# Recurrence of a diffusion step: decay factors made at a job's head, keys and queries projected first, their rotation spread over three jobs

## What is computed

```
h    = x * (1 + scale) + shift                 # adaLN
proj = h @ w_in                                # 1024 -> 3584 columns
o_a  = differential attention of q, k, v       # q, k of the 512 tokens rotated (2-D axial)
o_b  = gelu(u) * (w_s @ layer_norm(gelu(v)))   # spatial gating, u and v from proj
o_c  = gated linear recurrence, two directions # below
x    = layer_norm(ALPHA * x + gate * (concat(o_a, o_b, o_c) @ w_out))
x    = layer_norm(ALPHA * x + gate * top-2 of 16 experts(x modulated))
```

```
o_t   = (q_t * exp(b_t)) @ S + sum over s <= t of (q_t * exp(b_t - b_s)) . k_s  i_s
S_new = exp(b_last) * S + sum over s of (k_s * exp(b_last - b_s)) i_s
```

## Time and profile before

| | |
|---|---|
| runs shown (us) | 2160.1, 2160.1, 3152.97; median 2160.1 |
| profiled execution | 2148.85 us, span 2147.0 us, mean granted clock 0.93 |
| busy share of the span | PE 85%, PEld 44%, DVE 34%, ACT 18%, POOL 14% |
| recurrence of the first layer | 134.8 to 407.5 us |
| recurrence of the second layer | 1176 to 1455 us |

### The profile page before, as it was taken

How to read it: one execution, slowest core, us unless ns; L and a number is a source line. 1 busy time by engine, 2 the same in 40 slices (tenths; PEclk the granted TensorE clock), 3 DMA queues, 4 the chain that set the end, 5 groups by cost and what they waited for, 6 DMA issues and landing times. The chain is left out here.

```text
span 2147.0 us, 20618 instructions
## 1 busy us (share of the span) xinstructions
PE 1825.3 (85%) x7528; PEld 939.9 (44%) x7528; DVE 736.3 (34%) x1179; ACT 379.5 (18%) x699; POOL 302.7 (14%) x348
## 2 busy tenths in 40 slices
PE   3998888787984999999799898877879399999993
PEld 1464544544552443344345455445544344434441
DVE  0035465366453111111150555545635511101105
ACT  1323112143110000000141421212420100000001
POOL 0011125400000000000130222271000000000005
PEclk9999999899985999999899999988989589999997
DMA  9321111364117877799603012107320496897943
GB/s 368 132 95 40 46 45 40 138 246 178 68 59 267 319 265 296 287 363 396 231 16 134 1 44 86 40 1 261 119 78 30 148 370 220 309 382 266 397 159 147
DMA packets 142087, 380.44 MB, mean 177 GB/s; under 512 B 9732, under 2 KB 15876, under 8 KB 135332
## 3 DMA queue, kind: packets, MB, share of 16 engines
q1 hardware_dynamic: 111840, 292.31, 36.3%
q10 hardware_dynamic: 21108, 55.36, 7.1%
q0 software_dynamic: 9040, 31.46, 4.0%
HBM read 343.65 MB, written 35.45 MB: 177 GB/s over the span
## 5 line engine op out<-in xcount | busy, mean ns | idle before, releaser
L847 PE MATMUL psum<-sb_arena 128*128 128x512 f32 (+1 forms) x1248 | 494.2, 596 | 10.4 <-DMA sb_arena<-w_up 9.0
L577 PE MATMUL psum<-sb_wA,sb_arena 128*128 128x512 f32 x800 | 379.4, 625 | 0.0
L847 PEld LDWEIGHTS psum<-sb_arena 128*128 128x128 f32 (+1 forms) x1248 | 192.9, 172 | 269.2 <-issue 257.3
L847 PE MATMUL psum<-sb_wA,sb_arena 128*128 128x512 f32 (+1 forms) x672 | 273.7, 604 | 7.1 <-DMA sb_wA<-w_up 4.4
L577 PEld LDWEIGHTS psum<-sb_wA,sb_arena 128*128 128x128 f32 x800 | 154.0, 200 | 173.6 <-issue 167.9
L1316 DVE TENSOR_TENSOR sb_arena<-sb_arena 128x320 f32<-128x320 f32 (+8 forms) x252 | 151.2, 637 | 42.2 <-POOL sb_arena L1253 27.7
L1839 DVE COPY sb_arena<-psum 128x1024 f32<-128x1024 f32 x32 | 39.2, 1225 | 343.8 <-PE psum L835 343.8
L1479 DVE COPY_PREDICATED sb_arena<-sb_masks,psum 128x640 f32<-128x640 uint8 x128 | 112.3, 878 | 124.8 <-PE psum L649 106.8
L847 PEld LDWEIGHTS psum<-sb_wA,sb_arena 128*128 128x128 f32 (+1 forms) x672 | 101.8, 168 | 114.9 <-issue 106.5
L568 PE MATMUL psum<-sb_arena,sb_wA 128*128 128x128 f32 (+1 forms) x512 | 143.2, 441 | 0.0
L807 PE MATMUL psum<-sb_wA,sb_arena 128*128 128x512 f32 x320 | 140.3, 599 | 0.0
(11 more groups left out here) (185 smaller groups left out, 1689.6 us busy)
## 6 DMA issues: line engine op xcount, KB each, us to landing
sb_arena<-w_gate SPq DMA_DIRECT2D x22, 2048.0 KB, 18.4
sb_arena<-w_down SPq DMA_DIRECT2D x22, 2048.0 KB, 15.9
sb_wA<-w_up SPq DMA_DIRECT2D x16, 2048.0 KB, 20.7
sb_arena<-w_up SPq DMA_DIRECT2D x16, 2048.0 KB, 16.8
sb_wA<-w_ada SPq DMA_DIRECT2D x13, 2048.0 KB, 7.5
sb_wA<-w_in SPq DMA_DIRECT2D x12, 2048.0 KB, 9.6
sb_arena<-w_ada SPq DMA_DIRECT2D x11, 2048.0 KB, 7.7
sb_wA<-w_gate SPq DMA_DIRECT2D x10, 2048.0 KB, 17.9
```

The source lines that it names most:

```text
L577: mm = pe.matmul(unit_bank(n), hT[:, k, t * P:(t + 1) * P], w[:, k, :], start=k == 0, stop=k == KD - 1)
L847: mm = pe.matmul(out[r, :], act_T[:, k, r], w[:, k, cs], start=k == 0, stop=k == kn - 1)
```

## The change

Factors: the subtraction stands at the head of a job, after the first two distances, and its result lies in `gpad` (or in the other `bsum` buffer); ACT makes the three exps after the second level's exp; DVE and POOL multiply at the end without a further wait, and POOL does so right after its last level product. PE's turning of the keys waits for one masked copy of the last level less; the wait for the second stands before the products that overwrite its bank. Projections: blocks in the order KA, QA, UV, VA; the query unit of job 2 stands ahead of that job's first wait. Rotation: sixteen halves, one after each level product of jobs 1 and 2 (seven each) and two in job 3. The norm's four steps stand between the levels of job 3.

```diff
 UNITS = [
-    *[[(n, 0, 0), (n + 1, 1, 1), (n + 2, 2, 2), (n + 3, 3, 4), (n + 4, 5, 6), (n + 5, 7, 8)] for n in (12, 18, 24)],
+    *[[(n, 0, 0), (n + 1, 1, 1), (n + 2, 2, 2), (n + 3, 3, 4), (n + 4, 5, 6), (n + 5, 7, 8)] for n in (12, 18)],
+    [(24, -1, -1)] + [(25, 0, 0), (26, 1, 2), (27, 3, 4), (28, 5, 6), (29, 7, 8)],
     [(30, 0, 0), (31, 1, 2), (32, 3, 4), (33, 5, 6), (34, 7, 8)]]
...
+        def factors(ci):
+            return gpad[:, :, 1:P + 1], bsum[:, 1 - ci % 2, :, 1:P + 1]
...
-                    nm, s_ = ("I", "F", "Q", "UV", "VA", "KA", "QA")[b], SLOT_OF[b]
+                    nm, s_ = ("I", "F", "Q", "KA", "QA", "UV", "VA")[b], SLOT_OF[b]
...
                     pair, dr = c % 2, c // 2
+                    projections(-1)
                     pe.wait_ge(k_ready, nth(l, 4, ci + 1))
...
                     pe.wait_ge(K_ready, nth(l, 32, 8 * ci + 8))
-                    pe.wait_ge(lv_acc, nth(l, 64, 16 * ci + 16))
+                    pe.wait_ge(lv_acc, nth(l, 64, 16 * ci + 15))
...
                     pe.wait_ge(ke_evac, nth(l, 4, ci + 1))
+                    pe.wait_ge(lv_acc, nth(l, 64, 16 * ci + 16))
...
                         act.activation(Eb[:, j % 2], Eb[:, j % 2], ACT.Exp).then_inc(E_ready, 1)
-                        if j and j - 1 in at:
+                        if j - 1 in at:
                             projected(at[j - 1])
-                    act.wait_ge(Q_ready, nth(l, 32, 8 * ci + 6))
-                    act.wait_ge(K_ready, nth(l, 32, 8 * ci + 6))
...
+                        if j == 1:
+                            act.wait_ge(d_fac, nth(l, 4, ci + 1))
+                            kfac, qfac = factors(ci)
+                            beta = bsum[:, ci % 2, :, 1:P + 1] if c < 2 else bsum[:, ci % 2, :, 0:P]
+                            a, b = (kfac, qfac) if c < 2 else (qfac, kfac)
+                            act.activation(a, a, ACT.Exp)
+                            act.activation(b, beta, ACT.Exp)
+                            act.activation(eB[:, c, :], bsum[:, ci % 2, :, P], ACT.Exp).then_inc(fac_ready, 1)
                     projected(at[6])
-                    act.wait_ge(D_ready, nth(l, 32, 8 * ci + 8))
-                    act.activation(Eb[:, 0], Eb[:, 0], ACT.Exp).then_inc(E_ready, 1)
-                    act.activation(eB[:, c, :], bsum[:, ci % 2, :, P], ACT.Exp).then_inc(E_ready, 1)
...
-                rotated_between = [1, 2, 3, 4, 6, 7]
+                halves = [(u, half) for u in (1, 2, 3, 4, 6, 7, 8, 9) for half in range(2)]
+                turns = {(1 + i // 7, i % 7 + 1): h for i, h in enumerate(halves)}
...
                         gp.tensor_tensor(Kb[:, j % 2], kf[:, c], Eb[:, (j - 1) % 2], ALU.mult).then_inc(K_ready, 1)
-                        if ci == 2 and j == 1:
+                        if j == NL:
+                            until(gp, fac_ready, nth(l, 4, ci + 1))
+                            until(gp, K_ready, nth(l, 32, 8 * ci + 7))
+                            gp.tensor_tensor(kf[:, c].rearrange("p (w t) -> p w t", w=NT), kf[:, c].rearrange("p (w t) -> p w t", w=NT),
+                                             factors(ci)[0], ALU.mult).then_inc(K_ready, 1)
+                        if ci == 3 and j == 1:
                             inv_sqrt(1, rstd, mv[:, :, 1])
-                        if ci == 3 and j < NL:
-                            rotate(rotated_between[j - 1])
-                    until(gp, E_ready, nth(l, 40, 10 * ci + (9 if c < 2 else 8)))
-                    until(gp, K_ready, nth(l, 32, 8 * ci + 7))
-                    gp.tensor_tensor(kf[:, c], kf[:, c], Eb[:, 0 if c < 2 else 1], ALU.mult).then_inc(K_ready, 1)
-                rotate(8)
-                rotate(9)
+                        if (ci, j) in turns:
+                            rotate(*turns[ci, j])
...
                     distance(ci, c, 1, Eb[:, 1]).then_inc(D_ready, 1)
+                    b0 = 1 if c < 2 else 0
+                    tt(factors(ci)[0 if c < 2 else 1], bsum[:, ci % 2, :, P:P + 1].to_broadcast([P, NT, P]),
+                       bsum[:, ci % 2, :, b0:b0 + P], ALU.subtract).then_inc(d_fac, 1)
...
-                        if ci == 2:
+                        if ci == 3:
                             gmlp_norm(j - 1)
                     take(NL)
-                    dr_()
-                    v.wait_ge(K_ready, nth(l, 32, 8 * ci + 7))
...
-                       ALU.subtract).then_inc(D_ready, 1)
-                    v.wait_ge(E_ready, nth(l, 40, 10 * ci + (8 if c < 2 else 9)))
-                    tt(qf[:, c], qf[:, c], Eb[:, 1 if c < 2 else 0]).then_inc(Q_ready, 1)
-                    v.wait_ge(E_ready, nth(l, 40, 10 * ci + 10))
+                    v.wait_ge(fac_ready, nth(l, 4, ci + 1))
+                    tt(w5(qf[:, c]), w5(qf[:, c]), factors(ci)[1]).then_inc(Q_ready, 1)
                     v.wait_ge(ds_mm, nth(l, 4, ci + 1))
```

More of the change, by code:

```diff
@@ L312, in build_program @@
         f_ready, g_ready, k_ready = sem("f_ready"), sem("g_ready"), sem("k_ready")
+        d_fac, fac_ready = sem("d_fac"), sem("fac_ready")
         D_ready, E_ready, Q_ready, K_ready = sem("D_ready"), sem("E_ready"), sem("Q_ready"), sem("K_ready")
@@ L693, in _ @@
                     if u % 5 == 0:
-                        pe.wait_ge(pjA, nth(l, N_PJA, 26 + u))
+                        pe.wait_ge(pjA, nth(l, N_PJA, AT[3 + u // 5, 0] + 1))
                     else:
@@ L1003, in projected @@
                         a = act.activation(qf[:, t, P:T], pb, ACT.Copy)
-                    elif b == 3:
+                    elif b == 5:
                         a = act.activation(uv[:, t, :], pb, ACT.Gelu_apprx_tanh)
-                    elif b == 4:
+                    elif b == 6:
                         a = act.activation(vv[5 if t == 0 else t], pb, ACT.Copy)
                     else:
-                        if n == 25:
+                        if n == AT[3, 0]:
                             act.wait_ge(x_spilled, l * 16 + 16)
-                        a = act.activation(nat(n - 25), pb, ACT.Copy)
+                        a = act.activation(nat(5 * (b - 3) + t), pb, ACT.Copy)
                     a.then_inc(pjA, 1)
-                    if t == 0 and b in (4, 5):
+                    if t == 0 and b in (3, 6):
                         act.wait_ge(pjA, nth(l, N_PJA, n + 1))
-                        name, src, done = ("new_v", vv[5], out_v) if b == 4 else ("new_k", nat(0), out_k)
+                        name, src, done = ("new_v", vv[5], out_v) if b == 6 else ("new_k", nat(0), out_k)
                         act.dma_start(bass.AP(A[name].tensor, l * 65536, [[512, P], [1, 512]]), src).then_inc(done, 16)
@@ L1215, in _, with rotate @@
                         add_shift(l - 1, t)
-                def rotate(u):
+                def rotate(u, half):
                     t = u % 5
-                    until(gp, pjA, nth(l, N_PJA, 26 + u))
-                    raw = nat(u)
+                    if half == 0:
+                        until(gp, pjA, nth(l, N_PJA, AT[3 + u // 5, t] + 1))
                     cos = cst[:, C_COS + (t - 1) * 64:C_COS + t * 64]
@@ L1224, in rotate @@
                     sn = sin.rearrange("p (a s e) -> p a s e", a=2, s=2)
-                    for half in range(2):
-                        part = raw[:, half * 256:half * 256 + 256]
-                        gp.drain()
[L1228 to L1238, removed]
-                rotated_between = [1, 2, 3, 4, 6, 7]
+                    part = nat(u)[:, half * 256:half * 256 + 256]
+                    gp.drain()
+                    for s_ in range(2):
+                        src = part.rearrange("p (g a s e) -> p g a s e", g=4, a=2, s=2)[:, :, :, 1 - s_, :]
+                        out = ropeb.rearrange("p (g a s e) -> p g a s e", g=4, a=2, s=2)[:, :, :, s_, :]
+                        gp.tensor_tensor(out, src, sn[:, :, s_, :].unsqueeze(1).to_broadcast([P, 4, 2, 16]), ALU.mult)
+                    gp.drain()
+                    p3 = part.rearrange("p (g d) -> p g d", g=4)
+                    gp.tensor_tensor(p3, p3, cos.unsqueeze(1).to_broadcast([P, 4, 64]), ALU.mult)
+                    gp.drain()
+                    gp.tensor_tensor(part, part, ropeb, ALU.add)
+                    if half:
+                        gp.drain()
+                        gp.sem_inc(r_ready, 1)
+                halves = [(u, half) for u in (1, 2, 3, 4, 6, 7, 8, 9) for half in range(2)]
+                turns = {(1 + i // 7, i % 7 + 1): h for i, h in enumerate(halves)}
                 for ci, c in enumerate(JOBS):
@@ L1249, in _ @@
                     for j in range(1, NL + 1):
-                        until(gp, E_ready, nth(l, 40, 10 * ci + j))
+                        until(gp, E_ready, nth(l, 28, 7 * ci + j))
                         if ci or j > 1:
@@ L1426, in gmlp_norm @@
                     if step == 0:
-                        until(v, pjA, nth(l, N_PJA, AT[3, 4] + 1))
```

(10 more changed lines are left out.)

6 lines of the change are left out of this document (1 added, 5 removed).

## The result

The changed kernel took **2103.5 us** (median of 4 runs, 2098.4 to 2105.2); its time is **0.9756 of the time before, 95% interval 0.9735 to 0.9776** (the run of 3152.97 us among those of before is left out of the ratio). The forecast was 2098 in a range of 2084 to 2128. The profiled execution took 2098.44 us; its span fell from 2147.0 to 2096.6, by 50.4 us, where the sum had said 62.2.

A forecast was written before the change was run, and what follows sets the result against it. PE, busy 85% of the span, was taken to bound the kernel; 62.2 us saved in both layers' recurrence turned the profiled 2148.85 into 2086.6, and 11.2 for the median gave 2098 us, range 2084 to 2128.

The forecast's parts named there:

- The ends: Ends of jobs in the recurrence: 11.3 us for jobs 0 and 2, 11.1 for backward jobs, from 12.17 to 18.32.
- the first rival: Job 3's levels again take 54.02 and 56.34 us and its end keeps the low clock; 2119 us, chance 0.17.
- Job 2's front: From the last output product to job 2's level 7: 45.2 us instead of 52.31, gain 7.1 in the first layer.
- The rotation in jobs 1 and 2: Beside levels of jobs 1 and 2: POOL's loop with a half 4.3 to 5.3 us, jobs stay on PE's time.
- The order of the projections: Projections beside the recurrence: reordering, with Gelu beside job 2, costs nothing; otherwise one 1.28 us load a level is late.
- The head: Head of jobs 0, 1 and 3: the subtraction ahead of DVE's first product of queries costs 0.85 us a job.
- Job 3: Job 3's levels: 48.0 us instead of 54.02, with 5.4 idle before level 2; bounds of the gain nothing and 14.
- Contention: DVE's three products per level beside the rotation: 2.09 us instead of 1.63, 0.46 more, hidden by 1.26 to spare.
- The rival of exclusion: Short levels of jobs 1 and 2: DVE waits for POOL's instructions, 2.6 us a loop, 27 in all; 2125, chance 0.11.
- Job 3 gives it back: Power and half rotation meet DVE's work, so job 3's levels and end stay slow; 2119 us, chance 0.17.
- POOL bounds jobs 1 and 2: Short levels of jobs 1 and 2: POOL's loop takes 7.76 us against PE's 4.95; 2184 us, chance 0.05.
- The gain stops at the recurrence's end: Behind the recurrence: an unmoved load would be waited for, so the whole gains nothing; 2160 us, chance 0.04.

The follow-up runs named there:

- the last experiment: The changed kernel with PE's turning of the keys waiting for both masked copies of the last level again, instead of the first only: 2124.1 us.

## Why the prediction was right, and where its sum was off

**The ends: right.** 11.36 and 11.11 against 11.3 and 11.1, all at full clock, with a wait of 1.16 where about 1.2 was named; job 3's end too, which the first rival had kept slow. Leaving the factors at the end, or waiting for the second copy, brings slow ends back. **Job 2's front: right**, 45.06 against 45.2. **The rotation in jobs 1 and 2: right**, no wait of PE in the short levels. **The order of the projections** cost nothing that shows: job 2, beside which Gelu now stands, has PE busy all through. No run changed that order by itself.

**The head: 1.70 instead of 0.85.** The step priced the instruction that moves, 0.78 us, and not what it pushes: DVE's product of queries came after the start of POOL's key product and lost 0.92 us to it. Jobs 0 and 1 in two layers: 8.43 to 10.13 and 9.03 to 10.80, 3.5 us more than the sum had.

**Job 3: 52.1 and 52.5 instead of 48.0.** The mechanism came as told, up to level 2: it starts 10.78 + 9.32 = 20.10 us after level 0 (20.2 forecast), waiting for POOL behind the power and a half rotation. That the time agrees so well is luck: the chain began 0.9 late by the head, and the half rotation took 2.4 us (from the power's end to 332.46) instead of 3.47. The wait is 2.70, not 5.4, since PE itself came 2.6 us later than forecast: 0.9 by the head, the rest by the clock of 0.51 after the head's wait. In layer two, where that level ran at full speed, the wait is 4.28 and level 2 starts at 20.43. The levels after it were too cheap in the sum: 8.96 instead of 5.9, 6.58 instead of 5.5 twice. The kernel before, in job 2:

```profile
282.64 1.70 DVE L1319 TENSOR_SCALAR sb_arena<-sb_arena,sb_small 128x256 f32<-128x256 f32 x5
284.25 0.82 DVE L1316 TENSOR_TENSOR sb_arena<-sb_arena 128x640 f32<-128x640 f32 x1
```

In the first of these levels, the norm's five instructions take 3.84 us instead of some 1.7 and the product 1.94 instead of 0.82, both beside POOL: 3.2 us. In the other two the product takes 1.94: 1.1 each. So 3.1 + 2 x 1.1 - 1 (the allowance for the clock, already inside the 20.10) - 0.1 = 4.2, and 52.2. What failed was taking these DVE times from rows in which POOL was idle (busy 0.00 from 282.64 to 285.07).

**The whole sum.** 62.2 less job 3 (4.1 + 4.5) less heads (3.5) = 50.1; measured 50.4. The sum was 11.8 us too good, and the forecast of 2098 only 5.5 below the median: by luck, the median lay 11.2 us above the profiled execution before the change and 5.0 after it. The lower end of the range was mis-added too: job 3 without its stall is 48.0 - 39.6 = 8.4 us better in each layer, 16.8 and not 14, so 2081.

**Contention: the row misled.** The prediction took 0.46 us for DVE's triple beside the rotation, from a loop in which DVE waited for POOL and so met it always at the same point; it measures 1.35 to 1.46 (2.98 and 3.09 less 1.63), near the 3 us for the triple that it had listed as a sign of being wrong. The rival of exclusion had named up to 2.6 and 27 us. DVE had not 1.26 but some 1.05 to spare, since 0.20 of its wait is a gap that stays without any wait; so its loop became 5.37 and 5.23 us (281.26, 286.63, 291.86) against 4.95, and PE saw nothing of it in job 2's levels. That DVE, ahead by part of a level when job 2's short levels begin, swallowed the rest is read from its waits (1.25, then none) and was not tried with a longer job. The mechanism of that rival holds where DVE has nothing to spare, at the heads and in job 3.

**The other rivals.** *Job 3 gives it back* was half true: its levels gained 1.9 and 3.9 us instead of 6.0 and 8.3, but its end kept the full clock. *POOL bounds jobs 1 and 2* did not happen; the run with two halves a level, a loop 2.8 us above the level, shows what it would have cost. That agrees with the condition of 2 us or more; no loop between it and that of one half was run. *The gain stops at the recurrence's end* did not happen: the span is shorter by all of the recurrence's 50.3 us.

## What to carry to other kernels

An instruction moved ahead of work that two engines start together costs its own time and, where it turns round which of them comes first, the wait for the other; so see what the other engine starts within the next us. The price of an overlap can't be taken from one phase of a loop: bound it by the full length of the other engine's instruction, and ask which engine has that much to spare. Work for an idle engine goes beside the stage where its partner has room (job 1's long levels here), not into equal portions.

## What was not expected of the hardware

Two-input products on DVE and POOL nearly exclude each other: 128x640 takes 0.82 alone on DVE and 1.94 beside POOL's, which itself takes 1.72 instead of 1.32. The norm's five 128x256 instructions, beside a half rotation and a key product, took 3.84 instead of 1.70, and 2.70 where the rotation was out of job 3. These read one tile and two columns; whether they lose the time by the same exclusion is not shown.

Equal waits of PE do not have equal effects on its clock. After 2.33 us at job 3's level 1 two microseconds were granted 0.51 (the 1.2 GHz level) and the level took 2.51; after 2.34 us at job 1's level 1 it took 1.39, full speed, and so did job 3's level 1 in layer two after 2.68 us. The wait of 2.23 us at the transposes has the same two outcomes in the last experiment. In each pair of the first layer PE had done the same work just before (at the heads a level of 1.39 and a unit of 7.13); what decides is open. Where the clock fell after such a wait, in the last experiment, the end or level took 1.5 to 1.7 us longer.
